# Gate and up weights of a routed expert loaded as one run of eight rows per partition

## The chip, the cores and the metric

The kernel runs on one core of one Trainium2 chip. The metric is the device time of one execution in microseconds (us); less is better. PE is the matrix engine (TensorE), DVE is VectorE, ACT is ScalarE, POOL is GpSimd, and SP is the engine that issues most of the loads.

## What is computed

A trunk of two layers over 256 context and 256 latent tokens, width 1024, all in float32. The first half of each layer (three kinds of attention) is not touched here. The second half is a mixture of experts:

```
u = adaLN(x)                                   # (tokens, 1024)
eidx, ew = route(u)                            # 8 of 64 experts for each token
for each routed expert e and its tokens xr:
    hdn = silu(xr @ w_gate[e]) * (xr @ w_up[e])    # w_gate, w_up: (1024, 256)
    y   = hdn @ w_down[e]                          # w_down: (256, 1024)
f = shared expert + sum over a token's 8 experts of weight * y
```

In layer 0 all 512 tokens are routed, in layer 1 the 256 latent ones.

## The kernel before

Each of the two layers ends in a phase of four stages: merge (which also makes `u`), route, experts, combine.

**Where the rows come from.** The merge stage makes `u` for a tile of 128 tokens on DVE (L1959). ACT copies it into `up` with its columns in another order (L1919) and stores it to `u_d` in DRAM (L1921). Then ACT moves PE's transposes of `u` (L1898) into `UT` (L1924), from which the router's matmuls (L2059) read. The copy and the move of the last tile stand before the router's matmuls.

**Blocks and turns.** The rows of an expert are worked on in blocks of up to 64 tokens. POOL gathers a block's rows from `u_d` (L2317), each token as two half rows of 512 columns on two partitions (the first halves on partitions 0 to 63, the second halves on 64 to 127), so one gather has 128 places. PE transposes four chunks of 128 columns (L2365), and ACT copies them to `XT` (L2424). PE multiplies by gate and up (L2405), ACT makes silu (L2432), DVE the product (L2509), PE transposes it (L2415), ACT copies it (L2439), PE multiplies by down (L2381), DVE copies the result (L2497), and POOL scatters it to `y_d` in DRAM (L2322). A turn of the loop takes the four weight slots: slots of 2, 1, 2, 1 blocks in layer 0 (six blocks a turn), of one block each in layer 1 (four a turn).

**Who runs ahead.** The gather of block b + 3 is issued by POOL in iteration b, after DVE has its indices (L2469), into one of two buffers. PE needs it two iterations later, after the gate and up products of block b + 2. The scatter of a block must have landed before DVE copies the result of the block two later (L2495, L2497). The last result of a turn is taken right after the one before it, so there the scatter has less time; DVE's next one-hot, and through it L2509 and PE's L2415 of the next turn, come behind.

**The weights.** SP loads each slot as soon as its users are done: gate and up once the gate and up products are made, down once the down products are (L2524 and L2527, each load of 1 MB). Four slots of 24 KB per partition hold them. A matrix's row number is read as (h, p, k) with h of 2, p of 128 partitions and k of 4: partition p gets rows 4p to 4p + 3 and 512 + 4p to 512 + 4p + 3, as two runs of 4 KB. The down matrix's row number is read as (p, k) with k of 2: one run of 8 KB for each partition. The order of the columns in `u_d` matches that of the gate and up rows. All DMAs, those that SP and ACT issue and those that POOL issues, are moved by the same 16 DMA engines; the profile calls SP's queue q1 and POOL's q0, and calls what an engine moves at a time a packet.

Of the kernel before, what the change touches and what calls it, by code (L numbers as in the profile page):

```python
# [17 lines left out]
ACT = mybir.ActivationFunctionType  # L18
# [4 lines left out]
KT = D // P  # L23
# [120 lines left out]
def trunk(nc, a, out, depth=DEPTH):  # L144
    with ExitStack() as ctx:
# [8 lines left out]
        def sem(name):  # L154
            if name not in taken:
                taken[name] = shared[len(taken)]
            return taken[name]
# [32 lines left out]
        def ar(off, *dims):  # L190
            n = int(np.prod(dims))
            v = AR[:, off:off + n]
            if len(dims) == 1:
                return v
            names = "abcde"[:len(dims)]
            return v.rearrange(f"p ({' '.join(names)}) -> p {' '.join(names)}", **{c: k for c, k in zip(names[1:], dims[1:])})
# [126 lines left out]
        def modulation(e, l, which, dst, s, segs):  # L323

            n = 0
            for i, w in enumerate(which):
                for g in segs:
                    e.dma_start(dst[:, g, i, :], mod_d[l, g:g + 1, w * D:(w + 1) * D].broadcast_to([P, D])).then_inc(s, 16)
                    n += 16
            return n  # L330
# [1478 lines left out]
        def root(e, i, s_var, s_std):  # L1809
            e.wait_ge(s_var, i + 1)  # L1810
            e.activation(sm(32 + i, 1), sm(17 + 4 * i, 1), ACT.Sqrt).then_inc(s_std, 1)  # L1811
# [10 lines left out]
        def stage_merge(l, t0):  # L1822

            nm = f"s_mg_"
            s_gp, s_sg, s_op, s_tm, s_mt, s_ld, s_yp, s_ye, s_var, s_std, s_nx, s_next, s_t1, s_u, s_tp, s_te, s_up = (
                sem(nm + x) for x in ("gp", "sg", "op", "tm", "mt", "ld", "yp", "ye", "var", "std", "nx", "next", "t1", "u", "tp", "te", "up"))
# [8 lines left out]
            up = ar(B0 + 4096 + 8192, 2, D)  # L1835

            mb, u, tmp = ar(ZW * NT, 2, 2, D), ar(4096, 2, D), ar(ZW * NT + 4096, 2, D)
# [63 lines left out]
            def act(e, ch):  # L1901
                modulation(e, l, (2,), GM, s_ld, range(t0 // 2, 2))
                for i, nm_ in enumerate(("ln1_g", "ln1_b")):
                    e.dma_start(LNB[:, i, :], a[nm_][l:l + 1, :].broadcast_to([P, D])).then_inc(s_ld, 16)
                for i in range(3 * KT):
                    e.wait_ge(s_gp, i + 1)
                    if i >= KT:

                        e.wait_ge(s_tm, i - KT + 1)
                    e.activation(SGb[:, i % KT, n0:T], PS[:, i % 2, n0:T], ACT.Sigmoid).then_inc(s_sg, 1)  # L1910

                e.wait_ge(s_op, 3 * KT)
                modulation(e, l, (3, 4), mb, s_next, range(t0 // 2, 2))
                for i, t in enumerate(tiles):
                    root(e, i, s_var, s_std)
                    e.wait_ge(s_u, i + 1)
                    if i >= 2:
                        e.wait_ge(s_ud[i % 2], 16 * (i // 2))
                    e.activation(up[:, i % 2, :].rearrange("p (h k q) -> p h k q", h=2, k=4), u[:, i % 2, :].rearrange("p (h q k) -> p h k q", h=2, k=4), ACT.Copy).then_inc(s_up, 1)  # L1919
                    e.wait_ge(s_up, i + 1)  # L1920
                    e.dma_start(u_d[t * P:(t + 1) * P, :], up[:, i % 2, :]).then_inc(s_ud[i % 2], 16)  # L1921
                    for g in range(2):
                        e.wait_ge(s_tp, 2 * i + g + 1)
                        e.activation(UT[:, 4 * g:4 * g + 4, t * P:(t + 1) * P],  # L1924
                                     PS[:, (2 * i + g) % 4, :].rearrange("p (k q) -> p k q", k=4), ACT.Copy).then_inc(s_te, 1)
# [35 lines left out]
            def pool(e, ch):  # L1961
                for i in range(KT, 3 * KT):
# [3 lines left out]
                    mt = i % KT  # L1966
                    e.tensor_tensor(MT[:, mt, n0:T], MT[:, mt, n0:T], TM[:, i % 2, n0:T], ALU.add).then_inc(s_mt, 1)
            return dict(act=act, pe=pe, dve=dve, pool=pool)


# [299 lines left out]
        def expert_slots():  # L2270

            return BIG[:, 27904 - 2 * 6144:27904 + 2 * 6144].rearrange("p (s n) -> p s n", s=SLOTS)
# [246 lines left out]
        def load_expert(sp, l, sl, x, hidden_done=lambda: None, down_done=lambda: None):  # L2519

            W, wl = expert_slots(), moe[l]["wl"][sl]
            hidden_done()
            for off, w in ((0, "w_exp_gate"), (2048, "w_exp_up")):
                sp.dma_start(W[:, sl, off:off + 2048].rearrange("p (h n) -> p h n", h=2),  # L2524
                             a[w][l, x].rearrange("o (h p k) n -> p (o h) (k n)", h=2, k=4)).then_inc(wl, 16)
            down_done()
            sp.dma_start(W[:, sl, 4096:6144], a["w_exp_down"][l, x].rearrange("o (p k) n -> p (o k n)", k=2)).then_inc(wl, 16)  # L2527

# [3 lines left out]
        def load_first_experts(sp, l, send_list):  # L2532


            if l < DEPTH - 1:
                send_list()

            later["rows_stored", l](sp)
            for sl in range(2):
                load_expert(sp, l, sl, slice(sl, sl + 1) if l == DEPTH - 1 else listed(sp, sl))  # L2540
            if l == DEPTH - 1:
                send_list()

        def load_experts(sp, l, done):

            m_ = moe[l]
            last = l == DEPTH - 1
            per_slot = blocks_of_slots(2 if last else 0)
            nb = sum(per_slot)
            sp.wait_ge(s_wfree, done)  # L2550
            for sl in range(2, SLOTS):
                load_expert(sp, l, sl, slice(sl, sl + 1) if last else listed(sp, sl))
            n = sp.value_load(NPAIR[0:1, 0:1], min_val=1, max_val=TURNS[last])
            with sp.Fori(1, n) as i:
                for sl in range(SLOTS):
                    b = sum(per_slot[:sl + 1]) - 1
                    load_expert(sp, l, sl, listed(sp, i * SLOTS + sl),
                                lambda: sp.wait_ge(m_["gu"][b % 2], i * (nb // 2) + (b // 2 + 2)),
                                lambda: sp.wait_ge(m_["y"][b % 2], i * (nb // 2) + (b // 2 + 1)))
# [265 lines left out]
```

## Time and profile before

| | us |
|---|---|
| median of 3 runs | 3012.02 |
| lowest, highest | 3002.78, 3014.65 |
| span of the profiled execution | 3019.0 |

The page of the profile gives the execution's span, from its first to its last instruction, and no other time of it. Busy times are shares of that span. In the slices a digit is the busy share of a fortieth of the span, in tenths. A line of waits says who waited for whom, how long together, how often, and the longest. "issue" as a releaser means that the profile shows nothing that the engine waited for; a wait for the landing of an expert's weights stands under it or under the load of the down weights.

### The profile page before, as it was taken

The page shows a single profiled execution, that of the slowest core. Times are in us where ns is not written, and L with a number is a line of the kernel's source. Part 1 is how long each engine was busy: PE and PEld are TensorE (multiplying, and loading weights), DVE is VectorE, ACT ScalarE, POOL GpSimd, SP SyncE. Part 2 cuts the span into 40 slices and gives each one's busy share as a digit, 9 for nine tenths or more (in the row PEclk, how much of TensorE's full clock was granted, in tenths as well). Part 3 has the DMA queues.
Part 4 walks back from the last instruction along what each step waited for, and adds up shares of the span by engine and source line. Part 5 has one row for each costly group of instructions (what it writes and reads, how often), then busy time and mean ns, then how long its engine had stood idle before and what let it go on. Part 6 is the DMA issues. An engine that isn't in the chain of part 4 may idle for free. (4 is left out here: it accounts for less than half of the span.)

```text
span 3019.0 us, 60082 instructions
## 1 busy us (share of the span) xinstructions
PE 2641.8 (88%) x23115; PEld 1574.5 (52%) x23115; DVE 1241.6 (41%) x3459; ACT 699.4 (23%) x1603; POOL 560.2 (19%) x556
## 2 busy tenths in 40 slices
PE   6988988799998899999999789888699788888885
PEld 4566546544446455555555345646587554444442
DVE  1044467500035555555555442457502433333334
ACT  1245444210001111111111214644200211111111
POOL 0010015100110223233223101014201022222221
PEclk8989988799998999999999889998899799899998
DMA  7178210021121899999999542010142699999995
GB/s 260 46 242 293 101 57 4 31 84 68 71 73 57 337 364 364 373 371 370 376 361 346 220 160 89 2 56 4 45 147 101 220 409 410 405 400 405 405 406 200
DMA packets 205965, 659.15 MB, mean 218 GB/s; under 512 B 28295, under 2 KB 40377, under 8 KB 188273
## 3 DMA queue, kind: packets, MB, share of 16 engines
q1 hardware_dynamic: 171132, 590.67, 51.4%
q0 software_dynamic: 28000, 50.64, 4.5%
q10 hardware_dynamic: 6676, 15.58, 1.5%
q8 instruction: 121, 1.98, 0.3%
q14 instruction: 36, 0.29, 0.0%
HBM read 648.07 MB, written 49.89 MB: 231 GB/s over the span
## 5 line engine op out<-in xcount | busy, mean ns | idle before, releaser
L2405 PE MATMUL PS<-BIG 128*64 128x256 f32 x5440 | 660.4, 398 | 72.8 <-issue 67.7
L2405 PEld LDWEIGHTS PS<-BIG 128*64 128x64 f32 x5440 | 410.0, 144 | 276.9 <-issue 111.5
L2317 POOL DMA_INDIRECT BIG<-u_d,IXG x176 | 180.2, 1024 | 863.1 <-DVE IXG L2469 840.6
L2381 PE MATMUL PS<-BIG 128*64 128x512 f32 x1360 | 329.3, 605 | 5.2 <-ACT BIG L2439 5.2
L1853 PE MATMUL PS<-UT,BIG 128*128 128x512 f32 (+1 forms) x768 | 254.1, 492 | 7.4 <-PEq L2777 4.3
L2432 ACT ACTIVATE BIG<-PS 64x256 f32<-64x256 f32 x170 | 63.8, 375 | 800.8 <-PE PS L2405 791.8
L1853 PEld LDWEIGHTS PS<-UT,BIG 128*128 128x128 f32 x768 | 146.8, 192 | 114.2 <-issue 104.1
L2322 POOL DMA_INDIRECT y_d<-BIG,IXS x174 | 177.2, 1018 | 64.7 <-issue 56.1
L2509 DVE TENSOR_TENSOR BIG<-BIG,PS 64x256 f32<-64x256 f32 x170 | 72.2, 425 | 264.6 <-ACT BIG L2432 224.6
L1940 DVE TENSOR_TENSOR BIG<-BIG,PS 128x512 f32<-128x512 f32 (+1 forms) x48 | 26.6, 554 | 366.0 <-PE PS L1866 366.0
L580 PE MATMUL PS<-BIG,UT 128*128 128x512 f32 (+5 forms) x480 | 161.8, 496 | 3.6 <-POOLq L2725 3.0
L1137 PE MATMUL PS<-UT,BIG 128*128 128x512 f32 (+1 forms) x384 | 160.0, 572 | 0.0
L2381 PEld LDWEIGHTS PS<-BIG 128*64 128x64 f32 x1360 | 82.5, 136 | 128.0 <-issue 119.9
L2456 DVE TENSOR_SCALAR BIG<-CB,BIG 128x64 f32<-128x64 f32 x562 | 143.7, 326 | 6.4
L2495 DVE COPY IXS<-IXV 128x1 int32<-128x1 int32 x170 | 26.1, 154 | 270.5 <-PE PS L2381 225.8
L1866 PE MATMUL PS<-BIG 128*128 128x512 f32 (+1 forms) x384 | 125.3, 487 | 1.5 <-PE PS L1853 1.2
L580 PEld LDWEIGHTS PS<-BIG,UT 128*128 128x128 f32 x480 | 89.2, 198 | 69.2 <-issue 64.1
L2365 PE MATMUL PS<-CB,BIG 128*128 128x128 f32 x688 | 113.7, 288 | 9.4 <-issue 9.0
L2497 DVE COPY BIG<-PS 128x512 f32<-128x512 f32 x170 | 117.5, 691 | 5.9
L2424 ACT ACTIVATE BIG<-PS 128x512 f32<-128x512 f32 x172 | 102.7, 597 | 45.4 <-PE PS L2365 41.8
L2365 PEld LDWEIGHTS PS<-CB,BIG 128*128 128x128 f32 x688 | 72.7, 141 | 75.7 <-issue 71.7
L1137 PEld LDWEIGHTS PS<-UT,BIG 128*128 128x128 f32 x384 | 73.9, 197 | 71.3 <-issue 69.1
(393 smaller groups left out, 3410.5 us busy)
## 6 DMA issues: line engine op xcount, KB each, us to landing
BIG<-in_w_exp_gate SPq DMA_DIRECT2D x136, 1024.0 KB
BIG<-in_w_exp_up SPq DMA_DIRECT2D x136, 1024.0 KB
BIG<-in_w_exp_down SPq DMA_DIRECT2D x136, 1024.0 KB
BIG<-in_w_ada SPq DMA_DIRECT2D x24, 2048.0 KB, 8.6
BIG<-in_w_in SPq DMA_DIRECT2D x22, 2048.0 KB, 8.3
BIG<-y_d SPq DMA_DIRECT2D x24, 1024.0 KB, 14.9
BIG<-in_w_out SPq DMA_DIRECT2D x4, 2048.0 KB, 7.8
BIG<-mod_d ACTq DMA_DIRECT2D x12, 512.0 KB, 5.9
```

Of the source, the lines that this page charges most:

```text
L580: m = e.matmul(PS[:, 6 + i % 2, 0:n], UT[:, k, t * P:(t + 1) * P], w[:, k, w0:w0 + n], start=k == 0, stop=k == KT - 1)
L1137: x = e.matmul(PS[:, m % 2, s0:], w[:, k, (m % 4) * P:(m % 4 + 1) * P], UT[:, k, s0:], start=k == 0, stop=k == KT - 1)
L1853: m = e.matmul(PS[:, i % 2, n0:T], w[:, k, (mt % 4) * P:(mt % 4 + 1) * P], UT[:, k, n0:T], start=k == 0, stop=k == KT - 1)
L1866: m = e.matmul(PS[:, 2 + i % 2, n0:T], w[:, k, mt * P:(mt + 1) * P], src[b][:, k, n0:T], start=k == 0, stop=k == 3)
L2317: e.indirect_dma_start(out=XG[:, q, :], out_offset=None, in_=u_d.rearrange("t (h n) -> (t h) n", h=2), in_offset=bass.IndirectOffsetOnAxis ...
L2322: e.indirect_dma_start(out=y_d.rearrange("t (h n) -> (t h) n", h=2), out_offset=bass.IndirectOffsetOnAxis(ap=IXS[:, q:q + 1], axis=0), in_ ...
L2365: mm = e.transpose(PS[:, q, k * P:(k + 1) * P], XG[:, q, k * P:(k + 1) * P], ident)
L2381: mm = e.matmul(PS[half(c), 5 + q, :], HT[:, q, k, :], W[:, sl, w:w + 512], start=k == 0, stop=k == 1)
L2405: mm = e.matmul(PS[half(c), 2 + q, 0:FE], xt, W[:, sl, w:w + FE], start=k + hf == 0, stop=k + hf == 4)
L2424: e.activation(XT[:, q], PS[:, q, :].rearrange("p (k n) -> p k n", k=4), ACT.Copy).then_inc(s("xt", q), 1)
L2456: mm = e.tensor_scalar(OH[:, t, :], cst("slotid"), DC[:, t:t + 1], RC[:, t:t + 1], ALU.is_equal, ALU.mult)
L2497: e.tensor_copy(YB[:, q, :], PS[:, 5 + q, :]).then_inc(s("ye", q), 1)
```

## The change

The rows of the gate and up matrices are given to the partitions as (p, k) with k of 8: partition p gets rows 8p to 8p + 7, one run of 8 KB. The stored columns of `u` follow: `up` now holds column 8q + k at place 128k + q, so its first half has k of 0 to 3 and its second k of 4 to 7. The slots, the gathers, the transposes and the products stay the same; the k-th chunk of a half row still meets the k-th row of that half.

```
-  e.activation(up[:, i % 2, :].rearrange("p (h k q) -> p h k q", h=2, k=4),
-               u[:, i % 2, :].rearrange("p (h q k) -> p h k q", h=2, k=4), ACT.Copy)
+  e.activation(up[:, i % 2, :].rearrange("p (k q) -> p k q", k=KT),
+               u[:, i % 2, :].rearrange("p (q k) -> p k q", k=KT), ACT.Copy)

   for off, w in ((0, "w_exp_gate"), (2048, "w_exp_up")):
-      sp.dma_start(W[:, sl, off:off + 2048].rearrange("p (h n) -> p h n", h=2),
-                   a[w][l, x].rearrange("o (h p k) n -> p (o h) (k n)", h=2, k=4)).then_inc(wl, 16)
+      sp.dma_start(W[:, sl, off:off + 2048], a[w][l, x].rearrange("o (p k) n -> p (o k n)", k=KT)).then_inc(wl, 16)
```

## Rows read from the trace of the kernel before

**Rows 1.** The page: busy times, and DMA in 40 slices.
```profile
PE 2641.8 (88%) x23115; PEld 1574.5 (52%) x23115; DVE 1241.6 (41%) x3459; ACT 699.4 (23%) x1603; POOL 560.2 (19%) x556
...
DMA  7178210021121899999999542010142699999995
```

**Rows 2.** Busy times by stretch: expert loops of layers 0 and 1.
```profile
core 0: us, PE busy (x) PEld busy (x) DVE busy (x) ACT busy (x) POOL busy (x), PEclk, DMA share, GB/s
1050.00:1600.00 550.00, 532.22 (x4134) 285.65 (x4130) 287.57 (x992) 102.53 (x247) 169.50 (x166) 1.00 0.96 367
2403.00:2953.00 550.00, 465.61 (x3274) 259.43 (x3274) 179.84 (x658) 81.21 (x195) 132.68 (x130) 0.92 1.01 405
```

**Rows 3.** Waits, 1050 to 1600 us: total us, times, longest.
```profile
DVE IXS L2495 <- DMA y_d<-BIG,IXS: 18.8, 11, 2.1
...
PE PS L2415 <- DVE BIG L2509: 15.3, 14, 1.1
...
PEld PS L2405 <- issue: 8.0, 28, 0.3
...
PEld PS L2365 <- DMA BIG<-u_d,IXG: 3.2, 7, 0.9
```

**Rows 4.** Waits, 2403 to 2953 us.
```profile
PE PS L2405 <- issue: 67.7, 28, 4.8
```

**Rows 5.** The page: issues of the experts' weights.
```profile
BIG<-in_w_exp_gate SPq DMA_DIRECT2D x136, 1024.0 KB
BIG<-in_w_exp_up SPq DMA_DIRECT2D x136, 1024.0 KB
BIG<-in_w_exp_down SPq DMA_DIRECT2D x136, 1024.0 KB
```

**Rows 6.** DMA queue q1, 2274.5 to 2278 us, then 1131.2 to 1133.2 us.
```profile
q1 hardware_dynamic: 357, 1.46, 101.5%
...
q1 hardware_dynamic: 101, 0.83, 99.2%
```

**Rows 7.** Timeline, 1108 to 1128 us: SP's loads, a gather, and its user.
```profile
1111.18 0.38 SPq L2524 DMA_DIRECT2D BIG<-in_w_exp_gate  x1
1111.65 0.42 SPq L2524 DMA_DIRECT2D BIG<-in_w_exp_up  x1
1111.97 1.02 POOL L2317 DMA_INDIRECT BIG<-u_d,IXG  x1 [3.97 <-DVE IXG L2469]
...
1120.23 0.42 PEld L2365 LDWEIGHTS PS<-CB,BIG 128*128 128x128 f32 x4 [0.38 <-DMA BIG<-u_d,IXG]
```

**Rows 8.** DMA queues, 1113.2 to 1116.8 us: packets, MB, share.
```profile
DMA packets 268, 1.19 MB, mean 331 GB/s; under 512 B 21, under 2 KB 21, under 8 KB 224
...
q0 software_dynamic: 7, 0.01, 2.6%
```

**Rows 9.** A gather, and DMA queue q1 from 1045.6 to 1047.8 us.
```profile
1044.36 1.03 POOL L2317 DMA_INDIRECT BIG<-u_d,IXG  x1 [3.99 <-DVE IXG L2469]
...
q1 hardware_dynamic: 236, 0.91, 101.8%
```

**Rows 10.** A gather in layer 1, and DMA from 2617.5 to 2620.8 us.
```profile
2616.26 1.01 POOL L2317 DMA_INDIRECT BIG<-u_d,IXG  x1 [13.24 <-DVE IXG L2469]
...
DMA packets 303, 1.29 MB, mean 392 GB/s; under 512 B 41, under 2 KB 41, under 8 KB 249
```

**Rows 11.** DMA queues, 1116.8 to 1120.0 us.
```profile
q1 hardware_dynamic: 271, 1.06, 85.0%
q0 software_dynamic: 146, 0.18, 16.2%
```

**Rows 12.** DMA queues, 1082.25 to 1083.25 us.
```profile
q1 hardware_dynamic: 35, 0.28, 65.7%
q0 software_dynamic: 34, 0.14, 33.8%
```

**Rows 13.** Groups of ACT's instructions by shape.
```profile
L1919 ACT ACTIVATE BIG<-BIG 128x1024 f32<-128x1024 f32 x6 | 12.5, 2076 | 31.5 <-DVE BIG L1959 31.5
...
L982 ACT ACTIVATE BIG<-BIG 128x1024 f32<-128x1024 f32 x6 | 6.0, 1054 | 0.0
```

More of the change, by code:

```diff
@@ L1918, in act @@
                         e.wait_ge(s_ud[i % 2], 16 * (i // 2))
-                    e.activation(up[:, i % 2, :].rearrange("p (h k q) -> p h k q", h=2, k=4), u[:, i % 2, :].rearrange("p (h q k) -> p h k q", h=2, k=4), ACT.Copy).then_inc(s_up, 1)
+                    e.activation(up[:, i % 2, :].rearrange("p (k q) -> p k q", k=KT), u[:, i % 2, :].rearrange("p (q k) -> p k q", k=KT), ACT.Copy).then_inc(s_up, 1)
                     e.wait_ge(s_up, i + 1)
```

## The prediction

> **What bounds the kernel now.** I read the page first: its busy line and slices say that TensorE (PE) is busy for 88% of 3019.0 us and that the DMA engines stand at nine tenths in two long stretches, the expert loops of layer 0 and of layer 1 [rows 1]. The table by stretch then parts the two [rows 2]. In layer 0 (1050 to 1600 us) PE is busy for 532.2 of 550 us at full clock, and DMA stands at 0.96 of its time beside it. In layer 1 (2403 to 2953 us) PE is busy for 465.6 us only, and DMA is at 1.01 with 405 GB/s. The waits say why [rows 3]: in layer 0 PE never stops for a weight (what stands before L2405 is 0.3 us at the longest), but it stops 14 times for VectorE's L2509, 15.3 us together, once per turn of the loop, and 7 times, 3.2 us, for a gather that is late. VectorE in turn waits 11 times, 18.8 us, for a scatter. In layer 1 PE waits up to 4.8 us at a time in front of L2405, where only the expert's weights can be missing [rows 4]. So layer 0 is set by PE, with gathers and scatters that land just in time; layer 1 is set by the rate of the weight loads. Each layer makes 136 / 2 / 4 = 17 turns, from the 136 loads of each matrix [rows 5].
>
> **Part 1: records of 8 KB for records of 4 KB.** A gate or up load goes from 256 records of 4 KB to 128 of 8 KB, which is how the down load is moved already. Price of each: in a stretch with nothing but 4 KB records, 357 took 101.5% of 16 engines in 3.5 us, so 0.1592 us each; with nothing but 8 KB records, 101 took 99.2% in 2 us, so 0.3142 us [rows 6]. Two small ones cost 0.3184 us, one large 0.3142: 4.2 ns less for 8 KB. An expert's gate and up loads are 256 / 16 = 16 large records on each engine: 67 ns per expert. Layer 1 waits for weights over some 64 experts (17 turns of 4, less the first): 64 x 0.067 = 4.3 us less. One record more or less in the 2 us stretch moves the price by 3 ns, so I keep 1 to 8 us. In layer 0 it gives nothing: PE does not wait for weights there.
>
> **Part 2: what shares the engines.** Gathers and scatters go through the software queue q0, the weights through q1, on the same 16 engines. Follow the gather issued at 1111.97 us, just after a gate and an up load [rows 7]. The transposes that need it start at 1120.23, after 0.38 us of waiting for it: it has no slack. Its first 3.6 us after issue and setup (from 1113.2) move 7 records of q0 and, of the 268 less the 21 small ones, 247 records of weights, 15.4 per engine [rows 8]. I looked whether this wait goes by records or by bytes. After the gather of 1044.36, with 4 KB records alone, it is 2.2 us and 0.91 MB, which is 222 records, 13.9 per engine [rows 9]. After that of 2616.26, in layer 1, it is 3.3 us, 1.29 MB and 303 - 41 = 262 records, 16.4 per engine [rows 10]. The bytes differ by 1.4 times, the records by less than 1.2: a gather stands behind some 15 records, whatever their size. Fifteen records of 8 KB take 15 x 0.314 = 4.7 us where 3.6 were measured: 1.1 us later.
>
> Then the gather's own records take turns with q1's. Between 1116.8 and 1120.0 q0 moved 146 records (9.1 per engine) and q1 271 (16.9) [rows 11]. Where the down load alone is beside it, turns are one for one, 35 records of 8 KB to 34 of q0 in 1 us [rows 12]. Strict turns would pass 9.1 x 0.314 = 2.9 us of large records where 16.9 x 0.159 = 2.7 us of small ones passed: +0.2 us. The same ratio as now would pass 16.9 x 0.314 = 5.3 us: +2.6 us. I take +0.4, near strict turns. With no slack at this gather, PE stalls 1.5 us more per turn, 17 x 1.5 = 25.5 us in layer 0. The lower end is 0 (the wait goes by bytes, and 3.6 us is already close to the 3.3 of the other mixed stretch); the upper is 1.1 + 2.6 = 3.7 us per turn, 63 us.
>
> The Trainium skill ("DMA: Bandwidth & Descriptors", section "Queues, rings and completion order") has an engine drain a whole packet, some 9 to 17 descriptors, before it turns to another queue. As the rows count records, turns here are one for one. By the page, each of the 9.1 turns could cost the difference of at least nine records, 9 x 0.155 = 1.4 us, and the stall would be many times mine; the trace does not bear that out for the down load, which has such records now.
>
> The other three gathers issued under load have more time (PE's 7 late ones in some 14 turns are about one for every second turn [rows 3]), so I take nothing for them. The scatter that VectorE waits for at the turn's end delays L2509 and through it PE's L2415 [rows 3]. It is issued when the last weights asked for are nearly all in and the next wait for a slot; what is queued is drained before it in either form. I take 0; the bounds are -0.1 us (the queue drains a little faster) and +1 us a turn, so -2 to +17 us. Behind that wait stand VectorE's next one-hot and L2509; ScalarE and PE wait on them.
>
> **Layer 1's gathers and scatters** are delayed as well, by up to 15 x (0.314 - 0.2), 1.7 us, plus turns. PE idles 84 us of 550 there [rows 2], 5 us for each of 17 turns, most of it before L2405 [rows 4], so a delay eats time that PE would spend waiting for weights: 0. If it falls beside that wait and not in it, 1 us a turn, 17 us, is the upper end.
>
> **Part 3: the copy L1919** reads every eighth element in place of every fourth. It takes 2.076 us for 1024 elements, against 1.054 us for L982 of that shape, read in order [rows 13]: spacing has doubled it already. Ends: 0, or doubled again, 2.1 us for each of two last tiles, where L1924 and the router's matmuls are queued behind it (4 us); the earlier tiles hide it behind VectorE's layer norm. It touches a new place for each element before and after; I take 0. The DMA out of it, L1921, is unchanged; SP issues as many loads as before.
>
> **Sum.** -4.3 + 25.5 + 0 + 0 = +21 us on the execution shown. The page gives its span, 3019.0 us, and no other time of it; that is 7 us above the median of 3012.02, and the three runs lie within 12 us. 21 / 3019 is 0.7%: 3012 + 21 = 3033 us.
>
> **Rivals.**
> A (this forecast), gathers of layer 0 late: 0.56. For it: the counts of [rows 8 to 10] and [rows 12]. Against it: three short stretches, and records of 8 KB were never alone for long.
> B, the other side: q0's wait goes by bytes, or a faster drain makes up for it. Layer 0 stays as it is and layer 1 gains 1 to 8 us, 3004 to 3011 us, say 3007: not slower. It decides if the stall added per turn is under 0.5 us (17 x 0.5 = 8.5, less 4.3). For it: the wait is 3.3 to 3.6 us in both mixed stretches. 0.28.
> C, layer 1 gains far more. Its loads also meet a limit in the queue, since half as many records would let SP run further ahead. All of PE's waits before L2405 are at stake; if a fifth of 84 us goes, the time is 3012 - 17 - 4 = 2991 us. Against it: DMA is never idle there (1.01). 0.08. The Trainium skill ("Perfetto Trace Analysis", section "DMA Optimizations") says that going from 2 KB to 4 or 8 KB pieces can raise throughput dramatically where the kernel is DMA-bound. That is this case. Here 4 KB records alone moved 1.46 MB in 3.5 us, 418 GB/s, and 8 KB ones 0.83 MB in 2 us, 414: no such gain is in sight.
> D, as A, and layer 1 becomes set by late scatters: 25.5 + 17 - 4 = +38, 3050 us or more. 0.08.
> That nothing changes at all is in B: the copies are the same bytes.
>
> **How the numbers follow.** The predicted time is A's, 3033 us; its own range is 3012 to 3071 (a stall of 0.3 to 3.7 us per turn). The range over the cases is 2999 to 3066: it takes in B, D and nearly all of A and leaves out C and A's far end. Half a per cent, 15 us, is about what a measurement of this kernel can tell from no change: 2997 and 3027. Chances: slower by more: most of A (0.42) and D, 0.50. Faster by more: C and a little of B, 0.09. Within: 0.41.
>
> **What the profile after would show.** The 4 KB records of q1 in both loops are gone, and their number in all falls by 272 x 128, 34,800. Right in its steps: in layer 0 more wait at L2365 for the gather, about 1.5 us per turn in place of 3.2 us in all [rows 3], and a stretch after a gather's issue in which 15 records per engine of q1 pass in 4.7 us. In layer 1 the same waits before L2405, some 4 us shorter in sum. L1919 at 2.08 us. Wrong, if gathers in layer 0 land as soon as before (B), if layer 1's stretch shortens by over 10 us (C), or if PE waits there for L2509 in place of weights (D).

## The result

| | us |
|---|---|
| changed kernel, median of 20 runs | 3004.76 (2998.27 to 3012.29) |
| kernel before, median of 20 runs beside it | 3011.84 (3002.78 to 3016.91) |
| ratio | 0.9978, 95% interval 0.9969 to 0.9987 |
| span of the profiled execution, after | 3004.4 |

The change makes the kernel about 7 us faster, 0.22%. That is inside the half per cent that I called no change. The forecast of 3033 us had the wrong sign. What came is the time of rival B (3007 us), though not all of its mechanism.

### The profile after

The page. It has the same shape as before [rows 1]. The third line gives q1's packets: there were 171,132, so 34,816 fewer (272 loads of 128), as forecast.

```profile
PE 2634.4 (88%) x23115; PEld 1568.9 (52%) x23115; DVE 1239.9 (41%) x3459; ACT 698.9 (23%) x1603; POOL 560.8 (19%) x556
...
DMA  7178210022121899999999542010033599999995
...
q1 hardware_dynamic: 136316, 590.67, 50.9%
```

The same two stretches as in [rows 2]:

```profile
1050.00:1600.00 550.00, 537.63 (x4151) 287.46 (x4151) 288.05 (x996) 103.74 (x249) 168.65 (x165) 1.00 0.95 369
2403.00:2953.00 550.00, 471.75 (x3362) 262.47 (x3360) 183.37 (x669) 84.69 (x203) 135.77 (x133) 0.93 0.98 402
```

PE does more in both stretches than in [rows 2] (532.22 and 465.61 us). In layer 1 that is the change. In layer 0 it is not: the second profile of before, shown further down, has 539.97 us there.

Waits, 1050 to 1600 us, the lines that answer to [rows 3]:

```profile
PEld PS L2365 <- issue: 24.2, 63, 0.4
...
PEld PS L2365 <- DMA BIG<-u_d,IXG: 11.3, 20, 1.2
...
PEld PS L2405 <- issue: 8.9, 34, 0.3
PE PS L2415 <- DVE BIG L2509: 8.4, 14, 1.6
...
DVE IXS L2495 <- DMA y_d<-BIG,IXS: 1.5, 1, 1.5
```

The gather is late 20 times in 14 turns and not 7. But the total is 11.3 us, not the 21 (14 x 1.5) that I expected on top of 3.2.

Waits, 2403 to 2953 us, which answer to [rows 4]:

```profile
PEld PS L2405 <- issue: 85.3, 153, 4.0
...
PE PS L2405 <- issue: 63.4, 29, 4.0
```

The wait for layer 1's weights is 63.4 us where it was 67.7, and 4.0 us at the longest where it was 4.8.

The first and last gate or up product bound each layer's expert loop. These are the matmuls of L2405 in layer 0 and in layer 1 (count, ns at the least, in the middle and at the most, first and last start, shape), after:

```profile
L2405 PE MATMUL PS<-BIG x3264: 379/379/687, 1003.2 to 1675.9; 128*64 128x256 f32 x192
L2405 PE MATMUL PS<-BIG x2176: 379/379/689, 2397.8 to 2951.1; 128*64 128x256 f32 x198
```

So layer 0's loop takes 672.7 us and layer 1's 553.3. The profile shown of before has 676.1 and 562.7 (1009.5 to 1685.6, 2403.2 to 2965.9). This length is the measure for all that follows. Whole executions scatter by 10 us; for layer 1's loop the profiles of kernels with one record size agree within 0.9 us, and for layer 0's within 2 us, with one exception: the first profile of before, of which more below.

The copy, L1919, takes what it took, as forecast, 2.078 us against 2.076 [rows 13]:

```profile
L1919 ACT ACTIVATE BIG<-BIG 128x1024 f32<-128x1024 f32 x6 | 12.5, 2078 | 31.5 <-DVE BIG L1959 31.5
```

### The profile page after: what moved, and what is told of

Read it like the earlier page. It is cut to its first block and busy times, and to the rows that moved or that the text cites. A ratio compares the mean times of both kernels' runs of the same rounds, so it can differ in the third digit from the quotient of the medians.

```text
span 3004.4 us, 60082 instructions
## 1 busy us (share of the span) xinstructions
PE 2634.4 (88%) x23115; PEld 1568.9 (52%) x23115; DVE 1239.9 (41%) x3459; ACT 698.9 (23%) x1603; POOL 560.8 (19%) x556
## 5 line engine op out<-in xcount | busy, mean ns | idle before, releaser
L2405 PE MATMUL PS<-BIG 128*64 128x256 f32 x5440 | 659.0, 397 | 67.9 <-issue 63.4
L2405 PEld LDWEIGHTS PS<-BIG 128*64 128x64 f32 x5440 | 409.3, 143 | 270.7 <-issue 101.8
L2381 PE MATMUL PS<-BIG 128*64 128x512 f32 x1360 | 329.3, 605 | 5.2 <-ACT BIG L2439 5.2
L2509 DVE TENSOR_TENSOR BIG<-BIG,PS 64x256 f32<-64x256 f32 x170 | 72.2, 425 | 231.6 <-ACT BIG L2432 231.3
L2381 PEld LDWEIGHTS PS<-BIG 128*64 128x64 f32 x1360 | 82.4, 136 | 128.1 <-issue 119.9
L2365 PE MATMUL PS<-CB,BIG 128*128 128x128 f32 x688 | 113.7, 288 | 11.7 <-issue 8.8
L2365 PEld LDWEIGHTS PS<-CB,BIG 128*128 128x128 f32 x688 | 72.6, 141 | 78.6 <-issue 66.6
```

Source lines behind the costliest of these rows:

```text
L2365: mm = e.transpose(PS[:, q, k * P:(k + 1) * P], XG[:, q, k * P:(k + 1) * P], ident)
L2381: mm = e.matmul(PS[half(c), 5 + q, :], HT[:, q, k, :], W[:, sl, w:w + 512], start=k == 0, stop=k == 1)
L2405: mm = e.matmul(PS[half(c), 2 + q, 0:FE], xt, W[:, sl, w:w + FE], start=k + hf == 0, stop=k + hf == 4)
```

## The experiments

Three questions were open. Which layer gains, and which loses? Is layer 1's gain a price per record, a price of the changed row order, or a limit of the queue (rival C)? And does a gather's wait go by the number of weight records ahead of it, as my forecast had it, or not (rival B)?

Every kernel below computes the whole result. "Loops" are the lengths of the expert loops of layer 0 and layer 1, read as above, from one profile for each line. Each ratio is taken against runs of the kernel before made beside that kernel; their median is 3011.84 us for the changed kernel, 3010.04 for the 2 KB one and the three marked "again", and 3011.11 for the rest.

| kernel | ratio, 95% interval | median, us | loops, us |
|---|---|---|---|
| before, first profile | | 3011.84 | 676.1, 562.7 |
| before, second profile | | | 667.0, 562.7 |
| changed | 0.9978, 0.9969 to 0.9987 | 3004.76 | 672.7, 553.3 |
| changed, again | 0.9988, 0.9977 to 1.0000 | 3005.93 | 672.9, 553.5 |
| 8 KB in layer 0 only | 1.0021, 1.0011 to 1.0031 | 3016.57 | 671.9, 562.5 |
| the same, again | 1.0015, 1.0006 to 1.0024 | 3013.36 | 671.3, 562.7 |
| 8 KB in layer 1 only | 0.9978, 0.9968 to 0.9988 | 3003.35 | 668.9, 553.7 |
| the same, again | 0.9981, 0.9972 to 0.9990 | 3004.49 | 668.5, 554.2 |
| new order, 4 KB records | 1.0005, 0.9996 to 1.0014 | 3012.10 | 667.5, 563.1 |
| new order, 2 KB records | 1.0081, 1.0067 to 1.0096 | 3033.51 | 668.0, 581.3 |
| new order, 1 KB records | 1.0193, 1.0174 to 1.0211 | 3070.05 | 670.4, 617.9 |

### One layer at a time

The two edits are made under a condition on the layer, with before's forms in the other branch; the second kernel has `l == 1` in its place.

```
+  if l == 0:
+      e.activation(up[:, i % 2, :].rearrange("p (k q) -> p k q", k=KT), u[:, i % 2, :].rearrange("p (q k) -> p k q", k=KT), ACT.Copy).then_inc(s_up, 1)
+  else:
+      e.activation(up[:, i % 2, :].rearrange("p (h k q) -> p h k q", h=2, k=4), u[:, i % 2, :].rearrange("p (h q k) -> p h k q", h=2, k=4), ACT.Copy).then_inc(s_up, 1)
...
+  if l == 0:
+      sp.dma_start(W[:, sl, off:off + 2048], a[w][l, x].rearrange("o (p k) n -> p (o k n)", k=KT)).then_inc(wl, 16)
+  else:
+      sp.dma_start(W[:, sl, off:off + 2048].rearrange("p (h n) -> p h n", h=2),
+                   a[w][l, x].rearrange("o (h p k) n -> p (o h) (k n)", h=2, k=4)).then_inc(wl, 16)
```

Expected of 8 KB records in layer 0 only:

> The changed rows and columns in layer 0 alone, layer 1 as before. Theory 1 (the gain is layer 1's loop, which waits for weights; layer 0's loop is set by TensorE, and its later gathers are paid for by earlier scatters): the same time as before, within 3 us, 3009 to 3015. Theory 2 (layer 0's loop gains as well, by the 3.4 us that its two profiles differ by): 3 to 4 us faster. Theory 3 (late gathers cost layer 0 something, which layer 1's gain hid): 3 to 8 us slower.

Expected of 8 KB records in layer 1 only:

> The changed rows and columns in layer 1 alone, layer 0 as before. Theory 1: the whole gain of the change, 7 us or a little more faster than before, and layer 1's loop 9 us shorter. Theory 2: about 4 us faster. Theory 3: 10 to 15 us faster, more than the whole change gives.

Measured: 1.0021 and 0.9978. The edit costs time in layer 0 (5.5 us by the medians, 3016.57 against 3011.11) and gains it in layer 1 (7.8 us, 3003.35 against 3011.11), and each edit leaves the other layer's loop alone: 562.5 us in the first kernel, and 668.9 in the second, at the upper end of the 667.0 to 668.9 that four profiles with 4 KB records in layer 0 show (all but the first profile of before). Waits of the kernel with 8 KB in layer 0 only, 1050 to 1600 us (L2368 is L2365 moved by three lines):

```profile
PEld PS L2368 <- issue: 25.4, 66, 0.4
...
PEld PS L2368 <- DMA BIG<-u_d,IXG: 11.2, 18, 1.6
```

The same of the kernel with 8 KB in layer 1 only:

```profile
PEld PS L2368 <- issue: 30.4, 79, 0.4
...
PEld PS L2368 <- DMA BIG<-u_d,IXG: 2.3, 5, 0.6
```

The late gathers come and go with layer 0's edit. Both lines have to be read together: a wait of some 0.4 us stands before these transposes anyway (the line "issue"), and when the gather ends last, all of it moves to the gather's line. The sum goes from 32.7 to 36.6 us in 14 turns.

### The halves and the whole once more

The product of the first two ratios is 0.9999, while the whole gave 0.9978. Before explaining that gap I ran all three again, beside one another.

Expected of the changed kernel:

> The changed kernel again, beside its two halves on the same chip. If the halves add up, its ratio to the kernel before is the product of theirs: by the first runs 1.002 x 0.998 = 1.000. If the first runs of the halves were off by chance, it is 0.9978 as measured at first, and the layer-0 half comes out nearer to 1.000 or the layer-1 half nearer to 0.996 this time.

Expected of layer 1 only:

> The change in layer 1 alone, again. Its layer-1 loop was 9.1 us shorter in its profile than in that of the kernel before, which is 0.30% of 3012 us: 0.9970 expected, 0.9978 if the first measurement holds. If layer 0's half costs time, this one is the fastest of the three.

Expected of layer 0 only:

> The change in layer 0 alone, again. If late gathers cost layer 0 time that earlier scatters do not give back, 1.001 to 1.002; if it is neutral, 1.000.

Measured: 0.9988, 0.9981 and 1.0015, with the loops of the table. The product is 0.9996, and the whole's interval, 0.9977 to 1.0000, holds it. The loops had said so at once: the changed kernel has the layer-0 loop of the one (672.7 to 671.9) and the layer-1 loop of the other (553.3 to 553.7). So the loops show no gap; the one between the first ratios is most likely scatter of whole executions.

### The profile that I started from

The first profile of before has a layer-0 loop of 676.1 us, longer than that of any kernel above, with or without the edit. One more execution of the same kernel, a single one:

> The kernel before, one more profile. In the profile shown first its layer-0 loop takes 676 us, from the first to the last matmul of gate and up; the kernels that leave layer 0 as it was took 667.5 to 669 us. If that first profile was an unusually slow execution, this one shows 667 to 670 us, turns of 39.4 us, and some 8 to 9 us of waits of TensorE's L2415 for L2509. If it is a property of the kernel, it shows 675 us again, turns of 39.9 us and 15 us of those waits. Layer 1's loop: 562.5 us either way.

Its span is 3007.0 us, and its loops (L2405 again) are 667.0 and 562.7 us:

```profile
L2405 PE MATMUL PS<-BIG x3264: 379/379/687, 1004.5 to 1671.5; 128*64 128x256 f32 x192
L2405 PE MATMUL PS<-BIG x2176: 379/379/689, 2391.1 to 2953.8; 128*64 128x256 f32 x198
```

Its waits from 1050 to 1600 us, beside [rows 3]:

```profile
PEld PS L2365 <- issue: 28.9, 75, 0.4
...
DVE IXS L2495 <- DMA y_d<-BIG,IXS: 10.9, 7, 1.8
...
PE PS L2415 <- DVE BIG L2509: 7.8, 14, 0.9
PEld PS L2365 <- DMA BIG<-u_d,IXG: 3.2, 8, 0.5
```

PE's wait for L2509 is 7.8 us here against 15.3 in [rows 3]. In the ten other profiles it is 7.7 to 10.8 us, so half of the 15.3 belonged to one execution and not to the kernel. Of the 14.6 us between the spans 3019.0 and 3004.4, 9.1 us (676.1 - 667.0) are such a difference. Whoever compares only the two profiles finds a gain in layer 0 (676.1 to 672.7) where there is a loss.

### The size of the records alone

These kernels keep the changed row order and cut each partition's run into 2, 4 or 8 records for each matrix, with gate's and up's pieces alternating in the slot so that they can't be joined again. Compute, bytes, copy and gathers are those of the changed kernel. The edit for two records of 4 KB, from the changed kernel (four of 2 KB: r of 4 and k of 2; eight of 1 KB: r of 8 and k of 1):

```
-  w = c * 2048 + hf * 1024 + k * FE
+  r, j = divmod(4 * hf + k, 4)
+  w = (2 * r + c) * 1024 + j * FE
...
-  sp.dma_start(W[:, sl, off:off + 2048], a[w][l, x].rearrange("o (p k) n -> p (o k n)", k=KT)).then_inc(wl, 16)
+  sp.dma_start(W[:, sl, 0:4096].rearrange("p (r m n) -> p r m n", r=2, m=2)[:, :, off // 2048, :],
+               a[w][l, x].rearrange("o (p r k) n -> p (o r) (k n)", r=2, k=4)).then_inc(wl, 16)
```

Expected of 4 KB:

> Rows and columns in the changed order, so a partition reads one run of 8 KB from DRAM, but gate and up lie interleaved in the slot, and so each run lands as two records of 4 KB. If the number of records is what the change saves, this is the time of before, within 3 us. If the order in DRAM is what helps (one run, not two pieces 512 KB apart), it is 6 to 8 us faster than before, like the whole change.

Expected of 1 KB:

> The changed order with records of 1 KB (2048 of them for gate and up). By a fixed cost of some 9 ns a record (what is left when 0.1592 us of 4 KB and 0.3142 of 8 KB are put on one line is 4 ns; records of 8 bytes show 9), an expert's loads take 96 x 4 to 9 ns = 0.4 to 0.9 us more on each engine than with 4 KB, so layer 1's loop grows by 25 to 60 us. For the gathers: if a gather stands behind some 15 records whatever their size, its first data come 1.25 us + 15 x 0.05 us = about 2 us after its issue, and layer 0 waits for no gather; if it stands behind some 75 KB per engine, or a fixed time, they come 3 to 4.5 us after its issue, as before.

Expected of 2 KB:

> The changed order with records of 2 KB. Turns of layer 1 took 33.7 us with 8 KB records, 34.2 with 4 KB and 37.6 with 1 KB, so (37.6 - 34.2) / (4 x 96) = 8.9 ns for each further record on an engine. With 2 KB an engine gets 32 records more per expert than with 4 KB: 4 x 32 x 8.9 ns = 1.1 us, turns of 35.3 us, and 17 x 1.1 = 19 us on the whole kernel, about 3030 us. If the price is not linear (records under some size being dearer), turns stay near 34.2. First data of gathers in layer 1 are expected 4.4 us after their issue, as with 8, 4 and 1 KB.

**The order is free.** With 4 KB records the changed order takes before's time: 1.0005, loops of 667.5 and 563.1 us. So the effect of the change is that of the size of its records, as far as these measurements can tell.

**The price is one per record.** The layer-1 loop takes 553.7 us with 8 KB records (mean of four profiles), 562.7 with 4 KB (mean of five), 581.3 with 2 KB and 617.9 with 1 KB (one profile each). L2406 is L2405 moved by one line; 2 KB, then 1 KB:

```profile
L2406 PE MATMUL PS<-BIG x2176: 379/379/689, 2392.9 to 2974.2; 128*64 128x256 f32 x198
L2406 PE MATMUL PS<-BIG x2176: 379/379/689, 2399.4 to 3017.3; 128*64 128x256 f32 x198
```

The loop has 17 x 4 = 68 experts. SP issues the loads of the first two over 40 us ahead of it (in the changed kernel at 2353.27 and 2355.59 us, the next two at 2393.96 and 2395.30), so those of 66 fall into it, all but a few microseconds' worth. Halving the records adds 16, 32 and then 64 per engine and expert:

| step | loop, us | records more per engine | ns each |
|---|---|---|---|
| 8 to 4 KB | +9.0 | 16 x 66 = 1056 | 8.5 |
| 4 to 2 KB | +18.6 | 32 x 66 = 2112 | 8.8 |
| 2 to 1 KB | +36.6 | 64 x 66 = 4224 | 8.7 |

The records themselves say the same. The packed traces hold each record of q1 with its duration (no view prints them one by one); from 2400 to 2950 us the median is 312 ns for 8 KB (changed kernel), 160 for 4 KB, 85 for 2 KB and 47 for 1 KB (the three kernels of this section). Two halves take 8, 10 and 9 ns more than one whole.

A limit in the queue (rival C) would make one of these steps stand out. None does. SP is held up all the same: with 4 KB records its issues of a load take up to 5.52 us near 2600 us. SP's timeline, before:

```profile
2595.43 3.85 SPq L2524 DMA_DIRECT2D BIG<-in_w_exp_up  x1
2599.40 3.84 SPq L2527 DMA_DIRECT2D BIG<-in_w_exp_down  x1
...
2632.17 5.52 SPq L2527 DMA_DIRECT2D BIG<-in_w_exp_down  x1
```

And after:

```profile
2604.41 0.33 SPq L2526 DMA_DIRECT2D BIG<-in_w_exp_down  x1
...
2624.57 0.55 SPq L2524 DMA_DIRECT2D BIG<-in_w_exp_up  x1
```

In the whole loop the longest issue is 5.55 us before and 0.73 after. SP is no longer held up, as rival C said, but the engines had work all that time, and the even price per record leaves no room for a gain from it.

**A gather does not stand behind a number of records.** After the gather in layer 1 of the changed kernel, the DMA queues from 1.0 to 4.2 us behind its issue:

```profile
2646.80 1.02 POOL L2317 DMA_INDIRECT BIG<-u_d,IXG  x1 [3.98 <-DVE IXG L2469]
```

```profile
DMA packets 193, 1.36 MB, mean 424 GB/s; under 512 B 27, under 2 KB 27, under 8 KB 28
...
q1 hardware_dynamic: 184, 1.35, 101.4%
```

Of 193 packets 165 are of 8 KB, 10.3 per engine, and they hold 1.36 MB. Before it was 16.4 per engine and 1.29 MB in 3.3 us [rows 10]. With 1 KB records, from 1.25 to 4.25 us behind a gather's issue:

```profile
2600.65 1.02 POOL L2317 DMA_INDIRECT BIG<-u_d,IXG  x1 [4.94 <-DVE IXG L2470]
```

```profile
DMA packets 654, 1.07 MB, mean 356 GB/s; under 512 B 16, under 2 KB 596, under 8 KB 596
...
q1 hardware_dynamic: 654, 1.07, 104.7%
```

There is no packet of q0 yet, and 654 - 16 = 638 weight records have passed, 40 per engine. Ten, sixteen or forty records: the wait is about as long, and the bytes are alike (1.36, 1.29 and over 1.07 MB). The landings say the same over 60 gathers each. From the DMA view of 2403 to 2903 us, q1's packets, MB and share, and the gathers' count and median us from issue to landing, after:

```profile
q1 hardware_dynamic: 26206, 190.82, 92.5%
...
BIG<-u_d,IXG POOLq DMA_INDIRECT x61, 6.8
```

With 4 KB records in the new order:

```profile
q1 hardware_dynamic: 41118, 188.04, 93.8%
...
BIG<-u_d,IXG POOLq DMA_INDIRECT x60, 6.6
```

With 1 KB records:

```profile
q1 hardware_dynamic: 120064, 169.84, 98.1%
...
BIG<-u_d,IXG POOLq DMA_INDIRECT x55, 6.9
```

4.6 times the packets, and the median landing moves by 0.1 us (between 4 and 1 KB by 0.3).

The first data can be read for many gathers too, from the single records in the traces: those of layer 1's loop with no record of q0 shortly before, and q1 busy until the first group of q0's comes. With 8 KB records (changed kernel, 19 gathers) the median is 4.2 us behind the issue and 11 records of q1 per engine, with 4 KB (new order, 24 gathers) 4.3 us and 17, with 2 KB (31 gathers) 4.3 us and 32, with 1 KB (34 gathers) 3.8 us and 26 (up to 72: the 8 KB records of the down loads stand among the small ones). It is a wait under load and not the time of a gather by itself: behind the changed kernel's gather of 2948.59 us, when the loads are over, q0's first packets come between 2950.1 and 2950.6 us.

Whether under load the wait is one for bytes or for a fixed time these runs don't settle, since the engines move bytes at nearly one rate in all of them; the 2.2 us and 0.91 MB of [rows 9] fit neither as a constant.

## Why the prediction was wrong

**The step that failed: "a gather stands behind some 15 records, whatever their size."** I had two explanations, records and bytes, and three stretches with one size of record in the majority; 1.2 against 1.4 times decided it. That was too little, and the window's length is part of both counts. What the runs showed in its place: 9 to 11, 16 and 40 records per engine passed in a wait of about the same length. The place that answers to [rows 7] and [rows 8] in the changed kernel is the gather of 1107.63 us and the transposes that use it:

```profile
1107.63 1.02 POOL L2317 DMA_INDIRECT BIG<-u_d,IXG  x1 [3.98 <-DVE IXG L2469]
...
1116.45 0.42 PEld L2365 LDWEIGHTS PS<-CB,BIG 128*128 128x128 f32 x4 [0.94 <-DMA BIG<-u_d,IXG]
```

DMA queues from 1108.9 to 1112.3 us:

```profile
DMA packets 159, 1.16 MB, mean 342 GB/s; under 512 B 17, under 2 KB 17, under 8 KB 17
...
q1 hardware_dynamic: 158, 1.16, 91.7%
q0 software_dynamic: 1, 0.00, 0.0%
```

The wait is 3.4 us and 142 large records, 8.9 per engine; I had said 15 in 4.7 us. Before it was 15.4 records in 3.6 us. In place of the 1.1 us more of my sum stand 0.2 us less.

**Turns one for one: the small part that holds.** Rival B's landing as before is not quite what happened either. The next 3.2 us, 1112.5 to 1115.7 us, against [rows 11]:

```profile
q1 hardware_dynamic: 147, 1.06, 84.4%
q0 software_dynamic: 116, 0.16, 16.2%
```

q1's bytes are the same (1.06 MB) in half as many packets, 147 for 271, and q0 got 116 packets in where it had 146. So the gather's own records do go slower. From issue to use it is 8.8 us now and was 8.3 us before [rows 7], 0.56 us more: 0.2 less up to the first data and 0.7 more behind them, where I had +0.4.

The turns can be seen in the traces' single records, whose starts and durations string them end to start into 16 chains, one per engine (a reconstruction; the traces don't name the engine). From 1050 to 1600 us of the changed kernel q0 follows q1 8491 times, and 6982 times (82%) exactly one record of q1 stands between two of q0's.

**Its size in the loop.** PE's weight loads at L2365 wait, gather's line and "issue" together, 32.1, 32.7, 32.5 and 32.3 us in the four kernels and profiles with 4 KB records in layer 0 (the last has no line for the gather), and 35.5, 36.6, 34.0 and 36.6 us in those with 8 KB: 3.3 us more in 14 turns, 0.24 us per turn. For the loop of 672 us that makes 4.0 us, and the loop is 4.2 us longer (672.2 against 668.0, means of four; the 676.1 of the first profile of before is left out as the odd one, and with it the difference would be 2.6). That layer 0 loses does not hang on this choice: 8 KB in layer 0 only was slower both times, by 5.5 and 3.3 us. I had forecast 1.5 us per turn and 25.5 us. It also stays below the 0.5 us per turn from which rival B was said to decide.

**The term that was mis-sized: 4.2 ns per 8 KB.** The mechanism was right, in its place and in the count of records, but the price is 8.5 ns for this step (8.5 to 8.8 over the three) and the gain 9.0 us, not 4.3; it is above even the 8 us of my upper end. [Rows 6] gave the difference of two durations of 0.16 and 0.31 us from 101 and 357 packets, and I wrote myself that one record shifts it by 3 ns. The 0.3142 us is a little dear: the loop's median 8 KB record takes 312 ns, where its 4 KB one takes 160.

The Trainium skill ("Perfetto Trace Analysis", section "DMA Optimizations") says that going from 2 KB to 4 or 8 KB can raise throughput dramatically in a kernel bound by DMA. In layer 1's loop the runs give 3.2% for 2 to 4 KB (581.3 to 562.7) and 1.6% for 4 to 8 KB (562.7 to 553.7): the direction agrees, the word does not.

The Trainium skill's rule of whole packets ("DMA: Bandwidth & Descriptors", section "Queues, rings and completion order"), by which I estimated at least 1.4 us for each of q0's turns, would have made PE's stall over 10 us per turn of the loop (9.1 x 1.4). It is 0.24 us, and the chains above show q0 getting in after a single record 82% of the time. The trace does not show turns of whole packets here.

**What held.** Layer 0's PE does not wait for weights in either form, and layer 1's does. L1919 costs nothing. Layer 1's gathers show no cost in the loop's length, which follows the price of the records, though they land in 6.8 us in the median where 4 KB records gave 6.6. The scatter at the turn's end costs nothing: VectorE waits less for it (10.9 us in the second profile of before, 1.5 after), and PE's wait for L2509 is unchanged, 7.8 and 8.4 us. VectorE's wait for scatters falls, roughly, as the records grow: 1.4 to 5.9 us in the four profiles with 8 KB in layer 0, 10.9 to 18.8 in the five with 4 KB, 17.6 with 2 KB and 27.3 with 1 KB. Only with 1 KB does PE's wait for the product behind it grow, and layer 0's loop with it (670.4 us):

```profile
DVE IXS L2496 <- DMA y_d<-BIG,IXS: 27.3, 14, 2.1
...
PE PS L2416 <- DVE BIG L2510: 10.8, 14, 0.9
```

Why VectorE waits less with large records is not settled. In part the wait has only changed its name: its wait for PE's L2381 at the same copy rises from 126.6 to 134.8 us, so the two together are 137.5 and 136.3. A scatter itself takes longer, 7.7 us in the median where it took 6.9 (6.5 with 2 KB, 6.2 with 1 KB). From the DMA view of 1050 to 1600 us, the second profile of before:

```profile
BIG<-u_d,IXG POOLq DMA_INDIRECT x84, 6.8
y_d<-BIG,IXS POOLq DMA_INDIRECT x83, 6.9
```

And after:

```profile
BIG<-u_d,IXG POOLq DMA_INDIRECT x83, 6.7
y_d<-BIG,IXS POOLq DMA_INDIRECT x82, 7.7
```

**The sum as measured.** +4.2 us in layer 0 and -9.0 in layer 1 make -4.8 us. The whole kernel gave -7.1 and -4.1 us by its medians, layer 0 alone +5.5 and +3.3, layer 1 alone -7.8 and -5.6.

**The best version.** 8 KB in layer 1 only is 4.2 us better by the loops. Timed whole (0.9978 and 0.9981, against 0.9978 and 0.9988) its intervals overlap those of the change, so that this lead rests on the profiles alone.

## What to carry to other kernels

Where the landing of weights sets the end, count the records that each engine moves, and price them from whole loops of versions that differ in the size alone; a difference of two durations read in windows of 2 to 4 us is not a price. Larger records help only there: where matmuls set the end and a second queue feeds them with no slack, the same edit costs a little. A choice between records and bytes wants stretches in which the two differ by far more than 1.2 against 1.4, and a wait that one profile shows wants a second one before it is multiplied by a number of turns.

## What the hardware showed unexpectedly

Each record of a load costs 8.5 to 8.8 ns on its DMA engine beside its bytes, by the loops' lengths, the same from 1 to 8 KB; the durations of single records give 8 to 10. That is some 2.8% of an 8 KB record's 0.314 us [rows 6]. A gather in the software queue under a full hardware queue lands in 6.6 to 6.9 us in the median (layer 1), whether 26,206 or 120,064 packets pass beside it in 500 us. It does not wait for a number of records, but once its own are moving they take turns with the other queue's mostly one for one.
